# Eleven norms in two halves of the tokens, turned by a product with a diagonal matrix, and other places for the state space tables

## What is computed

```
def rmsnorm(x, g):
    xf = x.astype(jnp.float32)
    y = xf * lax.rsqrt(jnp.mean(xf * xf, axis=-1, keepdims=True) + EPS) * g.astype(jnp.float32)
    return y.astype(x.dtype)
...
for i in range(DEPTH):
    xn = rmsnorm(x, norm_g[i, 0])
    ...
    x = x + m.astype(x.dtype)
    f = conv_gated_ffn(rmsnorm(x, norm_g[i, 1]), ffn_w_up[i], ffn_conv_w[i], ffn_conv_b[i], ffn_w_down[i])
    x = x + f.astype(x.dtype)
return rmsnorm(x, final_norm_g)
```

## Time and profile before

| | us |
|---|---|
| median of three executions | 1906.72 (1906.52 to 1910.63) |
| the profiled execution | 1909.1 |
| its span, first to last instruction | 1907.4 |
| PE busy | 1763.9 (92%) |
| DVE busy | 1232.3 (65%) |
| ACT busy | 852.9 (45%) |
| POOL busy | 462.8 (24%) |

### The profile page before, as it was taken

How to read it: one execution, slowest core, us unless ns; L and a number is a source line. 1 busy time by engine, 2 the same in 40 slices (tenths; PEclk the granted TensorE clock), 3 DMA queues, 4 the chain that set the end, 5 groups by cost and what they waited for, 6 DMA issues and landing times.

```text
span 1907.4 us, 27119 instructions
## 1 busy us (share of the span) xinstructions
PE 1763.9 (92%) x11362; PEld 1561.8 (82%) x11362; DVE 1232.3 (65%) x1695; ACT 852.9 (45%) x1082; POOL 462.8 (24%) x629
## 2 busy tenths in 40 slices
PE   7999999699993998889999999899989999999998
PEld 6878999488993973448999888799978888989997
DVE  5556667556873779986766655576776656655445
ACT  5445555345551530015554544455554445543444
POOL 1210549605994017760000011200003200000000
PEclk9999999799996998999999999999999899999999
DMA  7434556444663551114555443455544522445551
GB/s 243 130 103 141 180 197 202 162 155 153 236 217 110 183 183 66 66 67 155 178 181 194 155 133 111 129 182 199 177 154 149 184 91 87 136 163 187 183 193 45
DMA packets 201531, 293.89 MB, mean 154 GB/s; under 512 B 6241, under 2 KB 162081, under 8 KB 199361
## 3 DMA queue, kind: packets, MB, share of 16 engines
q1 hardware_dynamic: 197568, 272.25, 43.2%
q0 software_dynamic: 2688, 11.51, 1.9%
q10 hardware_dynamic: 1152, 8.39, 1.2%
HBM read 282.70 MB, written 9.44 MB: 153 GB/s over the span
## 4 chain that ended last, share of the span: by engine, by line
PE 67%; POOL 13%; DVE 12%; ACT 4%; issue 3%; DMA 1%; SPq 0%; DVEq 0%; ACTq 0%; POOLq 0%
PE ps L107 65%; POOL arena L119 12%; DVE arena L119 3%; DVE arena L131 3%; DVE wlo L119 2%; PE ps L110 2%; ACT whi L113 2%; ACT arena L113 1%; DVE arena L125 1%; DVE xres L119 1%; DVE arena L122 1%; DVE arena L137 0%; POOL sm L119 0%; DMA raw<-in_sb_w_qkv 0%; DMA arena<-in_ssm_b_im 0%
## 5 line engine op out<-in xcount | busy, mean ns | idle before, releaser
L119 DVE TENSOR_TENSOR wlo<-raw,whi 128x2048 fp32r<-128x2048 f32 x258 | 604.6, 2346 | 339.9 <-ACT whi L113 339.7
L107 PE MATMUL ps<-xh,whi 128*128 128x256 f32 x2288 | 655.4, 286 | 31.4 <-DVE wlo L119 29.5
L107 PE MATMUL ps<-xl,whi 128*128 128x256 f32 x2288 | 650.8, 284 | 0.0
L107 PE MATMUL ps<-xh,wlo 128*128 128x256 f32 x2288 | 650.5, 284 | 0.0
L113 ACT ACTIVATE whi<-raw 128x2048 fp32r<-128x2048 f32 x258 | 491.2, 1906 | 260.2 <-PE ps L107 240.0
L107 PEld LDWEIGHTS ps<-xh,whi 128*128 128x128 f32 x2288 | 442.9, 194 | 41.8 <-DVE wlo L119 29.7
L107 PEld LDWEIGHTS ps<-xl,whi 128*128 128x128 f32 x2288 | 442.7, 193 | 1.6
L107 PEld LDWEIGHTS ps<-xh,wlo 128*128 128x128 f32 x2288 | 442.4, 193 | 0.0
L119 POOL TENSOR_TENSOR arena<-arena 128x512 f32<-128x512 f32 (+4 forms) x250 | 237.6, 970 | 95.7 <-DVE arena L131 37.6
L107 PE MATMUL ps<-whi,oh 128*128 128x512 f32 (+1 forms) x640 | 250.1, 391 | 7.1 <-DVE ol L119 6.3
L107 PE MATMUL ps<-wlo,oh 128*128 128x512 f32 (+1 forms) x640 | 247.6, 387 | 0.0
(11 more groups left out here) (129 smaller groups left out, 1644.5 us busy)
## 6 DMA issues: line engine op xcount, KB each, us to landing
raw<-in_ffn_w_up SPq DMA_DIRECT2D x88, 1024.0 KB, 5.1
raw<-in_ffn_w_down SPq DMA_DIRECT2D x44, 1024.0 KB, 4.9
raw<-in_sb_w_qkv SPq DMA_DIRECT2D x24, 1024.0 KB, 5.2
raw<-in_w_ffn_in SPq DMA_DIRECT2D x22, 1024.0 KB, 5.1
raw<-in_w_in SPq DMA_DIRECT2D x19, 1024.0 KB, 5.1
raw<-in_w_ffn_out SPq DMA_DIRECT2D x11, 1024.0 KB, 4.9
raw<-in_sb_w_o SPq DMA_DIRECT2D x8, 1024.0 KB, 4.9
tabs<-arena POOLq DMA_DIRECT2D x8, 1024.0 KB, 5.3
```

What stands on the lines that cost most here:

```text
L107: return NOP if self.e is None else self.e.matmul(*a, **k)
L119: return NOP if self.e is None else self.e.tensor_tensor(*a, **k)
```

## The change

The final products of a stage are made for token half 0 first, then for half 1, and so are the additions and squares. After the third addition DVE makes half 0's sum, waits for its `pow` and builds a diagonal matrix, the identity times that factor (`rstd_dve(0)`); then it makes the last addition in two parts of 256 features. ACT squares the first of the two, DVE itself the second, and `rstd_dve(1)` makes the second diagonal matrix. PE multiplies each 128x128 block of `x` by the diagonal matrix of its half, which turns and scales it at once: eight products for half 0 as soon as its matrix is there, eight for half 1. The eight DVE operations of scaling go, and so does `jk` as their target. The norms turn into eight banks, one block each (`ple` into four as before), and TensorE's first product waits for the first `xl` alone. The `pow`s are two of one column for one of two. The double norm `second` gets the same in `final_rstd_dve`, with two `pow`s in series for each half.

On POOL T0 alone stays ahead of the `pow` of `gate`; T1 comes behind the gating's `pow`, and T2 to T7 behind the norm of `ffn1`.

```
@@ add_residual
-        for j in range(2):
-            for t in range(2):
-                if (t, j) != (1, 1):
-                    dv.wait_ge(*self.on("sum", st, t, j))
-                else:
-                    dv.wait_ge(*self.on("tile", *key))
-                xs = self.x[:, t, j * 512:(j + 1) * 512]
-                dv.tensor_tensor(xs, self.B[4 + 2 * t + j][:, :], xs, ALU.add).then_inc(*self.up("x_new", nxt, t, j))
+        for t in range(2):
+            for j in range(2):
+                xs, b = self.x[:, t, j * 512:(j + 1) * 512], self.B[4 + 2 * t + j]
+                if (t, j) == (1, 1):
+                    self.rstd(dv, nxt, 0)
+                    dv.wait_ge(*self.on("tile", *key))
+                    dv.tensor_tensor(xs[:, 0:256], b[:, 0:256], xs[:, 0:256], ALU.add).then_inc(*self.up("x_half", nxt))
+                    dv.tensor_tensor(xs[:, 256:512], b[:, 256:512], xs[:, 256:512], ALU.add).then_inc(*self.up("x_new", nxt, 1, 1))
+                else:
+                    dv.wait_ge(*self.on("sum", st, t, j))
+                    dv.tensor_tensor(xs, b[:, :], xs, ALU.add).then_inc(*self.up("x_new", nxt, t, j))
+        self.rstd(dv, nxt, 1)
@@ the norm on DVE (the old norm_dve goes)
+    def rstd_dve(self, dv, st, t):
+        ss, rs, dg = self.small("ss" + st, 5), self.small("rs" + st, 6), self.diag(st)
+        if t == 0:
+            dv.wait_ge(*self.on("squared", st, 0, 1))
+            dv.tensor_scalar(rs[:, 2:3], ss[:, 0:1], ss[:, 1:2], D * EPS, ALU.add, ALU.add).then_inc(*self.up("part", st, 0))
+        else:
+            xb = self.x[:, 1, 768:1024]
+            dv.wait_ge(*self.on("squared", st, 1, 0))
+            dv.tensor_scalar(rs[:, 4:5], ss[:, 2:3], D * EPS, None, ALU.add)
+            self.wait_x(dv, st, 1, 1)
+            dv.tensor_tensor_reduce(self.jk[:, 1, 768:1024], xb, xb, 1.0, 0.0, ALU.mult, ALU.add, ss[:, 4:5]).then_inc(*self.up("part", st, 1, 0))
+            dv.wait_ge(*self.on("part", st, 1, 0))
+            dv.wait_ge(*self.on("squared", st, 1, 1))
+            dv.tensor_scalar(rs[:, 3:4], ss[:, 4:5], ss[:, 3:4], rs[:, 4:5], ALU.add, ALU.add).then_inc(*self.up("part", st, 1))
+        dv.wait_ge(*self.on("rstd", st, t))
+        ...
+        dv.tensor_scalar(dg[:, t, :], self.ident[:, :], rs[:, t:t + 1], 32.0, ALU.mult, ALU.mult).then_inc(*self.up("scaled", st, t))
@@ norm_pe
-        for p in range(4):
-            pe.wait_ge(*self.on("scaled", st, p))
-            ...
-                    ins = pe.transpose(self.B[banks[p]][:, kk * 256 + t * P:kk * 256 + (t + 1) * P],
-                                       self.jk[:, t, kt * P:(kt + 1) * P], self.ident[:, :])
-            ins.then_inc(*self.up("x_turned", st, p))
         for t in range(2):
+            pe.wait_ge(*self.on("scaled", st, t))
+            for kt in range(KT):
+                b, c = self.turned_at(st, kt)
+                ...
+                ins = pe.matmul(b[:, c + t * P:c + (t + 1) * P], self.x[:, t, kt * P:(kt + 1) * P], dg[:, t, :], start=True, stop=True)
+                if t and kt % n == n - 1:
+                    ins.then_inc(*self.up("x_turned", st, kt // n))
@@ gpsimd
         self.s5_params_pool(po)
-        self.s5_tables_pool(po, range(0, 3))
-        self.norm_pool(po, "gate")
+        self.s5_tables_pool(po, range(0, 1))
+        self.rstd_pool(po, "gate")
         self.gating_pool(po)
-        self.norm_pool(po, "ffn1")
-        self.s5_tables_pool(po, range(3, 8))
+        self.s5_tables_pool(po, range(1, 2))
+        self.rstd_pool(po, "ffn1")
+        self.s5_tables_pool(po, range(2, 8))
```

More of the change, by code:

```diff
@@ L446, in wait_x, with bank_read, diag, norm_act @@
+    def bank_read(self, st, b):
+        if st == "ffn2":
+            return (b % 4) // 2, 1 - b // 4
+        return ((b - 4) // 2, b % 2) if b >= 4 else None
+    def diag(self, st):
+        return carve(self.ar, 2048, 2, P) if st == "second" else carve(self.ar, 8192, 2, P)
+    def wait_x(self, e, st, t, j, half=False):
         if st == "stick0":
             e.wait_ge(*self.on(f"x_in{t}{j}"))
+        elif half:
+            e.wait_ge(*self.on("x_half", st))
         else:
             e.wait_ge(*self.on("x_new", st, t, j))
[L451 to L456, removed]
+    def norm_act(self, ac, st, gcol, more=None):
+        ss = self.small("ss" + st, 5)
+        for t in range(2):
+            for j in range(2):
+                last = t == j == 1
+                c = slice(j * 512, 768 if last else (j + 1) * 512)
+                self.wait_x(ac, st, t, j, last)
@@ L499, in turned_dve @@
[L499 to L510, removed]
-            pe.wait_ge(*self.on("scaled", st, p))
[L512 to L516, removed]
-                    ins = pe.transpose(self.B[banks[p]][:, kk * 256 + t * P:kk * 256 + (t + 1) * P],
-                                       self.jk[:, t, kt * P:(kt + 1) * P], self.ident[:, :])
-            ins.then_inc(*self.up("x_turned", st, p))
+        self.turned_act(ac, st, gcol)
@@ new lines, in norm_pe @@
+    def norm_pe(self, pe, st):
+        banks, dg = self.norm_banks(st), self.diag(st)
+        n = KT // len(banks)
+        if st == "stick0":
+            self.gains_pe(pe)
+            pe.wait_ge(*self.on("gains"))
+        for t in range(2):
+            pe.wait_ge(*self.on("scaled", st, t))
+            for kt in range(KT):
+                b, c = self.turned_at(st, kt)
+                read = self.bank_read(st, banks[kt // n]) if st != "stick0" and t == 0 else None
+                if read:
+                    pe.wait_ge(*self.on("x_new", st, *read))
+                ins = pe.matmul(b[:, c + t * P:c + (t + 1) * P], self.x[:, t, kt * P:(kt + 1) * P], dg[:, t, :], start=True, stop=True)
+                if t and kt % n == n - 1:
+                    ins.then_inc(*self.up("x_turned", st, kt // n))
@@ new lines, in final_rstd_pool @@
+    def final_rstd_pool(self, po):
+        rs = self.small("rsf", 12)
+        for t in range(2):
+            r1, r2, m1, m2 = (rs[:, 6 * t + i:6 * t + i + 1] for i in range(4))
+            po.wait_ge(*self.on("part", "second", t, 0))
+            po.tensor_tensor(r1, m1, self.mhalf[:, 0:1], ALU.pow).then_inc(*self.up("fn_rstd", t))
+            po.wait_ge(*self.on("part", "second", t, 1))
+            po.tensor_tensor(r2, m2, self.mhalf[:, 0:1], ALU.pow).then_inc(*self.up("rstd", "second", t))
@@ L2375, in tensor @@
         self.tiles_used = 0
-        self.norm_pe(pe, "stick0", more=lambda: self.gains_pe(pe))
+        self.norm_pe(pe, "stick0")
         self.stick_pe(pe, "stick0", self.early_pe(pe))
```

213 lines of the change are left out of this document (117 added, 96 removed).

## The result

The changed kernel takes 1924.56 us (median of four executions, 1922.78 to 1927.76) where the kernel before takes 1908.06 beside it (four, 1906.52 to 1910.63): a ratio of 1.008 (95% interval 1.007 to 1.0095), **slower by 16.5 us**. The prediction was 1925.2. The profiled execution took 1924.64, its span 1922.9 against 1907.4, the mean granted clock 0.961 against 0.964.

The account below looks back on a forecast made before the run. Bound: a wait chain mostly on TensorE (67%), with GpSimd's tables holding up the gate power and ffn1's fetch, plus the norms. Tables +10.9, norms -2.35 and ple +9.9 sum to +18.45 on 1906.72: 1925.2 us, range 1910 to 1940.

Parts of the forecast that it names:

- Tables, +10.9: Moved GpSimd tables: earlier gate power, later fetch behind ffn1's norm and slower gating together cost +10.9 us.
- `gate` -14.0: Norm gate: with T0 alone ahead, GpSimd's power starts at about 352.4 and not 366.44, -14.0 us.
- The sixth table +21.9: Behind ffn1's norm: six tables for five make the ssm_b_im fetch 21.9 us later, lengthening VectorE's wait.
- the step that priced it by the one table in the idle time, 21.3: Behind ffn1: the added table priced like T7, which ran in VectorE's idle time, 21.3 us.
- The gating +3: Gating: T1 beside it delays VectorE operations reading two SBUF tiles, +3 us, between 0 and +6.
- `ple`, +9.9: Last norm: later projection start +6.4, half clock +1.7, uncovered diagonal products +1.8; together +9.9 us (8 to 12).
- The common norm: Worked in stick1: VectorE's new wait ahead of its last addition uses up the saving, 0.0 us (-0.5 to +0.5).
- -2.35: Summed effect of the norms other than ple, from -2.0 for ffn0 and s5 to +1.15 for ffn1: -2.35 us.
- The clock, no net effect: TensorE's clock in the norms: pause shortens to 2.2 us but stays, no net effect (-1 to +2 us a norm).
- rival B: Norms: half clock over both halves' products, +2 to +3 us in eight norms, 1943 us; chance 0.11.
- `second`, +1.0: Double norm second: four powers for two on VectorE's path, +1.0 us (-0.5 to +2.5).
- rival C: Norms: each diagonal product takes four of a transpose's passes, 0.44 us; +27 over ten norms, 1952 us; chance 0.03.

Follow-up runs that it names:

- experiment 8: Changed kernel with ple's diagonals behind its cuts, fillers, four tables ahead of ffn1's norm, and the last addition before the power wait: 1872.99 us, ratio 0.9812.
- experiment 6: Changed kernel with the tables where the kernel before has them and ple's diagonals made behind its cuts: 1909.58 us, ratio 0.9999.

## Why the prediction was right, and which terms were off

The sum was +18.45 on the profiled execution's time and came out at +15.5; against the medians, +18.5 and +16.5.

- **Tables, +10.9: right.** Alone they measured +10.7 by the profiled span and +8.6 by the medians. Its parts: `gate` -14.0, measured -14.6. The sixth table +21.9, measured +19.7 (49.15 less 29.46): the step that priced it by the one table in the idle time, 21.3, was near, but the last table ran faster there than T7 had (from its start at 578.9 to its transfer's issue 18.1 us, 20.7 before). The gating +3, measured +5.3: the step took 0.7 us on eight operations; four were hit, by 0.5 to 1.6 each, and the clock added its 1.5 behind the longer wait, which the step left out. The two errors cancelled.
- **`ple`, +9.9: right**, +10.3, by the predicted wait: TensorE's standstill ahead of the projection 8.10 us, foreseen at 8.0, and undoing it gave back 8.5.
- **The common norm: right in mechanism** (VectorE 0.66 idle behind its third addition, two records a product, the late power), and of +0.6 in price, as experiment 8 shows; a power and a diagonal were cheaper than their bounds (0.55 and 0.29 for 0.69 and 0.35). By the profiles the ten other norms gave back 7.0 (15.5 less 10.7 for the tables and 11.8 for `ple` and the end) where -2.35 stood; by the medians, 16.5 less 8.6 less 11.8, it is about 4. The difference is luck of single profiles: the stretch to `ffn4`, 250.86 in this one, was 253.76 in the other profile of the same program. In a comparison without the tables' places and `ple`'s late start the norms came to nothing, `ple` and the end with them (experiment 6).
- **The clock, no net effect: right on the mean, but for a wrong reason.** The prediction took the pause of 2.2 us for a pause like the 3.8 before. It is one in which the clock falls in one execution and not in the next. The five profiles with halves and no fillers have 16 standstills of 2.12 to 2.30 us in `gate`, `ffn1`, `ffn2` and `stick1`, and behind 7 of them it fell; in `ffn4` (2.13) it fell in 4 of 5. Some 0.4 to 1.2 us hang on it in a norm, so rival B came true in part, at about half of its price.
- **`second`, +1.0:** +2.06, inside its own bounds. Four powers in series stand ahead of the last addition and the second half (TensorE idle 4.59 us).
- **The end, +1.5, was not foreseen**: over their first 5 us the main products of `ple` have a clock of 0.66, and 1.00 in the kernel before; the sum had no term for it.

## What to carry to other kernels

Work that has no fixed place (here eight tables of 19 to 33 us on GpSimd) was worth more than the shape of a norm: list for each idle stretch of its engine how long it is and who waits behind it; two tables fewer behind `ffn1` took 39 us off TensorE's wait, and the norm in halves was worth 0 to 5. Splitting a reduction to start earlier puts a wait ahead of whatever is queued behind its first part: hand the sum over, do the queued work, and wait then. Where TensorE stands still for about 2 us between bursts, compare two profiles of the same kernel before explaining a difference of 1 us, or fill the pause with transposes of the identity.

## What the runs showed of the hardware that was not expected

- After the same standstill of 2.30 us the granted clock was 0.52 in one profile of a kernel and 1.00 in another; after 1.0 to 1.3 us (`ffn0`, `s5`, `ffn3`) the norm ran at 1.00 in all ten usable profiles of kernels with the halves. Eight diagonal products take 3.8 us from first start to last end at a clock of 0.50 (`second`) and 2.05 at 1.00.
- A VectorE subtraction of two SBUF tiles of 128x256 took 0.42 us alone, and 2.03, 1.55, 0.98 and 0.92 beside a GpSimd table.
- Each of the sixteen diagonal products takes two records (32 in `ple`, 3.73 us), a transpose of the same 128x128 one (16 in 1.91 us): twice, as the earlier trace rows said, and the prediction's rival C falls with it.
